# The dilated branch's projection moved ahead of the grouped-query heads

## What is computed

```python
def hybrid_mixer(h, ...):
    proj = h @ w_in                      # 1024 x 8192: dilated qkv | B's q, k, v | gates
    o_a = dilated attention, 3 groups x 8 heads of 64, merged by their log-sum-exp     # S x 512
    o_b = gqa_axial_attention(...)       # 8 query heads, 2 kv heads of 128: rmsnorm, axial rope,
                                         # softmax, values                              # S x 1024
    gates = sigmoid(pg + b_gate)         # S x 2 x 1024
    merged = gates[:, 0] * (o_a @ w_branch_a) + gates[:, 1] * (o_b @ w_branch_b)
    return merged @ w_out
```

## Time and profile before

| | us |
|---|---|
| median of 3 runs | 2217.85 |
| lowest, highest | 2215.59, 2220.27 |
| profiled execution, span from its first to its last instruction | 2216.1 |
| PE busy | 2087.5 (94%) |
| DVE busy | 1321.9 (60%) |
| ACT busy | 924.7 (42%) |
| POOL busy | 191.5 (9%) |
| chain that ended last: PE, DVE, ACT | 84%, 11%, 3% |

### The profile page before, as it was taken

How to read it: one execution, slowest core, us unless ns; L and a number is a source line. 1 busy time by engine, 2 the same in 40 slices (tenths; PEclk the granted TensorE clock), 3 DMA queues, 4 the chain that set the end, 5 groups by cost and what they waited for, 6 DMA issues and landing times.

```text
span 2216.1 us, 29141 instructions
## 1 busy us (share of the span) xinstructions
PE 2087.5 (94%) x12208; PEld 1800.8 (81%) x12208; DVE 1321.9 (60%) x1269; ACT 924.7 (42%) x866; POOL 191.5 (9%) x76
## 2 busy tenths in 40 slices
PE   8999999978999879999999999989989999699998
PEld 7987888876888657887988788879979878687997
DVE  6766656687666635656756666664454556444544
ACT  5344333365333433333335433343444445444433
POOL 0001000121000113001000200010010003311000
PEclk9999999979999999999999999999999999999999
DMA  8443555434554404554544455525446543243552
GB/s 309 153 166 138 209 189 190 157 114 152 190 189 166 158 22 167 190 189 152 209 152 177 154 192 189 190 95 207 182 156 227 146 136 117 74 153 124 187 208 98
DMA packets 32362, 364.16 MB, mean 164 GB/s; under 512 B 3677, under 2 KB 3938, under 8 KB 10130
## 3 DMA queue, kind: packets, MB, share of 16 engines
q1 hardware_dynamic: 28146, 347.49, 42.8%
q0 software_dynamic: 4128, 15.39, 2.7%
HBM read 361.77 MB, written 1.10 MB: 164 GB/s over the span
## 4 chain that ended last, share of the span: by engine, by line
PE 84%; DVE 11%; ACT 3%; issue 1%; DMA 0%; SPq 0%; DVEq 0%; ACTq 0%
PE acc L861 25%; PE bank L1262 10%; PE bank L821 9%; PE bank L823 9%; PE bank L822 9%; PE bank L1264 5%; PE bank L848 2%; PE bank L850 2%; PE bank L849 2%; DVE h L2151 2%; PE bank L1372 1%; PE bank L931 1%; PE bank L1021 1%; PE bank L814 1%; DVE h L2138 1%
## 5 line engine op out<-in xcount | busy, mean ns | idle before, releaser
L821 PE MATMUL bank<-ht_both,w_hi 128*128 128x256 f32 x1696 | 478.3, 282 | 7.0 <-DVE ob_lo L2661 6.8
L823 PE MATMUL bank<-ht_both,w_lo 128*128 128x256 f32 x1696 | 475.4, 280 | 0.0
L822 PE MATMUL bank<-ht_both,w_hi 128*128 128x256 f32 x1696 | 475.0, 280 | 0.0
L2078 DVE TENSOR_TENSOR w_lo<-raw,w_hi 128x4096 fp32r<-128x4096 f32 (+3 forms) x87 | 327.9, 3769 | 137.2 <-ACT w_hi L1525 136.9
L1513 ACT ACTIVATE w_hi<-raw 128x2048 fp32r<-128x2048 f32 x174 | 323.4, 1908 | 143.4 <-PE bank L823 138.6
L1262 PE MATMUL bank<-ht_both,w_hi 128*128 128x512 f32 x1024 | 359.7, 394 | 0.5
L1525 ACT ACTIVATE w_hi<-raw 128x4096 fp32r<-128x4096 f32 (+3 forms) x87 | 269.0, 3093 | 185.3 <-PE bank L1264 175.1
L821 PEld LDWEIGHTS bank<-ht_both,w_hi 128*128 128x128 f32 x1696 | 320.2, 189 | 12.2 <-issue 11.2
L822 PEld LDWEIGHTS bank<-ht_both,w_hi 128*128 128x128 f32 x1696 | 320.1, 189 | 1.6 <-issue 0.5
L823 PEld LDWEIGHTS bank<-ht_both,w_lo 128*128 128x128 f32 x1696 | 320.2, 189 | 0.0
L2073 DVE TENSOR_TENSOR w_lo<-raw,w_hi 128x2048 fp32r<-128x2048 f32 x98 | 220.1, 2287 | 115.4 <-ACT w_hi L1513 115.3
(11 more groups left out here) (325 smaller groups left out, 2999.9 us busy)
## 6 DMA issues: line engine op xcount, KB each, us to landing
raw<-slabs_in SPq DMA_DIRECT2D x147, 2048.0 KB, 7.7
raw<-slabs_in SPq DMA_DIRECT2D x23, 1024.0 KB, 6.3
raw<-slabs_in SPq DMA_DIRECT2D x12, 512.0 KB, 10.0
g_tab<-gains_in POOLq DMA_DIRECT2D x11, 512.0 KB, 6.5
a_bias<-bias_rows POOLq DMA_DIRECT2D x8, 576.0 KB, 6.9
b_tab<-gains_in POOLq DMA_DIRECT2D x8, 512.0 KB, 7.7
raw<-slabs_in SPq DMA_DIRECT2D x2, 1152.0 KB, 5.7
raw<-slabs_in SPq DMA_DIRECT2D x1, 1280.0 KB, 7.1
```

What stands on the lines that cost most here:

```text
L821: nc.tensor.matmul(o, whi, xhi, start=first, stop=False)
L822: nc.tensor.matmul(o, whi, xlo, start=False, stop=False)
L823: return nc.tensor.matmul(o, wlo, xhi, start=False, stop=last)
L2078: nc.vector.tensor_tensor(w_lo[slot][:, 0:w], raw[slot][:, 0:w], w_hi[slot][:, 0:w].bitcast(F32), ALU.subtract).then_inc(lo_ready, 1)
```

## The change

PE computes wa right after gates 0 to 3, ahead of bt and of branch B's heads, and puts it into the four accumulator banks, which stand in the list `bank` as numbers 4 to 7. There it stays until DVE reads it at the place where it did before. The slab of wa moves from place 16 to place 14; the slabs of gates 4 to 7 move from 14 and 15 to 15 and 16. ACT gets a second split between gates 3 and bt (slab 15), so that it splits slab 16 at head 0, 17 at head 4, 18 at head 7, and the split after the sigmoid goes. DVE's and POOL's lists are as before: POOL still makes the low parts of places 13 to 17, now gates, wa, gates, gates, wb.

```diff
--- before.py
+++ after.py
@@ -50,6 +50,7 1941.00:1947.00 6.00, 5.68 (x35) 5.71 (x36) 2.40 (x9) 1.02 (x4) 0.00 (x0) 0.72 0.73 303
 FFN_B = D_FF2 // 256
 A_G, A_H, A_HD = 3, 8, 64
 AV_SLAB = (3, 4, 8)
+GATE_SLAB = (12, 13, 15, 16)
 B_H, B_KV, B_HD = 8, 2, 128
 B_SCALE = B_HD ** -0.5
 SLAB = 4096
@@ -308,6 +309,7 1941.00:1947.00 6.00, 5.68 (x35) 5.71 (x36) 2.40 (x9) 1.02 (x4) 0.00 (x0) 0.72 0.73 303
         bank = [ctx.enter_context(nc.psum_tensor(f"bank{i}", [P, 512], F32)) for i in range(4)]
         acc = [[ctx.enter_context(nc.psum_tensor(f"acc{t}{n}", [P, 512], F32)) for n in range(2)]
                for t in range(TT)]
+        bank += acc[0] + acc[1]
 
 
         cst_loaded = sem("cst_loaded")
@@ -321,8 +323,8 1941.00:1947.00 6.00, 5.68 (x35) 5.71 (x36) 2.40 (x9) 1.02 (x4) 0.00 (x0) 0.72 0.73 303
         hi_ready = sem("hi_ready")
         lo_ready = sem("lo_ready")
         slab_used = sem("slab_used")
-        bank_full = [sem(f"bank_full{i}") for i in range(4)]
-        bank_read = [sem(f"bank_read{i}") for i in range(4)]
+        bank_full = [sem(f"bank_full{i}") for i in range(8)]
+        bank_read = [sem(f"bank_read{i}") for i in range(8)]
         acc_full = sem("acc_full")
         acc_half = sem("acc_half")
         acc_read = sem("acc_read")
@@ -410,7 +412,7 1941.00:1947.00 6.00, 5.68 (x35) 5.71 (x36) 2.40 (x9) 1.02 (x4) 0.00 (x0) 0.72 0.73 303
         BESIDE_M = {0: [("qn", 2), ("qr", 1)], 1: [("rot", 2)], 2: [("qn", 3), ("mv", 0, 1)], 3: [("mv", 1, 1)]}
 
 
-        uses = [0] * 4
+        uses = [0] * 8
         ticket = {}
         turn_of = [0]
 
@@ -535,6 +537,8 1941.00:1947.00 6.00, 5.68 (x35) 5.71 (x36) 2.40 (x9) 1.02 (x4) 0.00 (x0) 0.72 0.73 303
             take("ao", hd)
         for i in range(4):
             take("gt", i)
+        for i in range(4):
+            take("wa", i, slot=4 + i)
         for i in range(5):
             take("bt", i)
         take("bs", 0)
@@ -546,8 +550,6 1941.00:1947.00 6.00, 5.68 (x35) 5.71 (x36) 2.40 (x9) 1.02 (x4) 0.00 (x0) 0.72 0.73 303
             take("bp", hd)
             if hd % 2 == 0:
                 take("bo", hd // 2)
-        for i in range(4):
-            take("wa", i)
         for i in range(4):
             take("wb", i)
         take_transposes(2 * DEPTH + 2, aligned=True)
@@ -632,8 +634,8 1941.00:1947.00 6.00, 5.68 (x35) 5.71 (x36) 2.40 (x9) 1.02 (x4) 0.00 (x0) 0.72 0.73 303
             released[g0 + AV_SLAB[i]] = full("av", i, 1)
             released[g0 + 9 + i] = full("b", i, 1)
         for i in range(4):
-            released[g0 + 12 + i] = full("gt", 2 * i + 1)
-        released[g0 + 16] = full("wa", 3)
+            released[g0 + GATE_SLAB[i]] = full("gt", 2 * i + 1)
+        released[g0 + 14] = full("wa", 3)
         for i in range(2):
             released[g0 + 17 + i] = full("wb", 2 * i + 1)
         by_down([g0 + 19, g0 + 20], 2 * DEPTH + 2)
@@ -1345,9 +1347,10 1941.00:1947.00 6.00, 5.68 (x35) 5.71 (x36) 2.40 (x9) 1.02 (x4) 0.00 (x0) 0.72 0.73 303
                     tokens(("b", s, t), g0 + 9 + s, t, 512, KD, 512, 0, ht_hi, ht_lo)
 
                 def gates(i):
-                    need(g0 + 12 + i // 2)
+                    g = g0 + GATE_SLAB[i // 2]
+                    need(g)
                     c = i % 2 * 256
-                    up_pair(("gt", i), g0 + 12 + i // 2, (c, c + P), KD, 512, ht_hi, ht_lo)
+                    up_pair(("gt", i), g, (c, c + P), KD, 512, ht_hi, ht_lo)
 
                 def beside(hd, i):
                     if hd in BESIDE_A:
@@ -1412,6 +1415,11 1941.00:1947.00 6.00, 5.68 (x35) 5.71 (x36) 2.40 (x9) 1.02 (x4) 0.00 (x0) 0.72 0.73 303
 
                 for i in range(4):
                     gates(i)
+                need(g0 + 14)
+                for hd in range(A_H):
+                    pe.wait_ge(*read("ao", hd))
+                for i in range(4):
+                    up_pair(("wa", i), g0 + 14, (i * 256, i * 256 + P), 4, D, oa_hi, oa_lo)
                 for i in range(5):
                     key = ("bt", i)
                     wait_free(*key)
@@ -1458,11 +1466,6 1941.00:1947.00 6.00, 5.68 (x35) 5.71 (x36) 2.40 (x9) 1.02 (x4) 0.00 (x0) 0.72 0.73 303
                                              b_pt[hd % 2][:, kb * S:(kb + 1) * S], start=kb == 0, stop=kb == 1)
                     if hd % 2 == 1:
                         m.then_inc(bank_full[ticket["bo", hd // 2][0]], 1)
-                need(g0 + 16)
-                for hd in range(A_H):
-                    pe.wait_ge(*read("ao", hd))
-                for i in range(4):
-                    up_pair(("wa", i), g0 + 16, (i * 256, i * 256 + P), 4, D, oa_hi, oa_lo)
                 for i in range(4):
                     pe.wait_ge(*read("bo", i))
                 for s in range(2):
@@ -1955,7 +1958,7 1941.00:1947.00 6.00, 5.68 (x35) 5.71 (x36) 2.40 (x9) 1.02 (x4) 0.00 (x0) 0.72 0.73 303
                         .then_inc(b_std, 1)
                 for i in range(4):
                     gates(i)
-                    if i == 1:
+                    if i % 2 == 1:
                         split_one()
                 for i in range(5):
                     copy_bank(("bt", i), b_qk[:, 2 * i:2 * i + 2, :].rearrange("p a s -> p (a s)"))
@@ -1994,7 +1997,6 1941.00:1947.00 6.00, 5.68 (x35) 5.71 (x36) 2.40 (x9) 1.02 (x4) 0.00 (x0) 0.72 0.73 303
                     for i in range(4 * branch, 4 * branch + 4):
                         act.wait_ge(*read("gt", i))
                     nc.scalar.activation(gate[:, c, :], gate[:, c, :], ACT.Sigmoid).then_inc(gate_ready, 1)
-                split_one()
                 for s in range(2):
                     for i in range(2):
                         q = 2 * s + i
@@ -2847,8 +2849,9 1941.00:1947.00 6.00, 5.68 (x35) 5.71 (x36) 2.40 (x9) 1.02 (x4) 0.00 (x0) 0.72 0.73 303
                 parts += columns(qk) + [chunks(dil[:, 2, 0:2, half].reshape(D, 512))]
                 if half == 0:
                     parts.append(chunks(dil[:, 2, 2].reshape(D, 512)))
-            parts += columns(w[:, 3 * A_G * 512:])
-            parts += rows(a["w_branch_a_2"][0]) + columns(a["w_branch_b_2"][0]) + rows(a["w_out_2"][0])
+            own = columns(w[:, 3 * A_G * 512:])
+            parts += own[0:5] + rows(a["w_branch_a_2"][0]) + own[5:7]
+            parts += columns(a["w_branch_b_2"][0]) + rows(a["w_out_2"][0])
     widths, _ = slab_widths()
     slabs = np.zeros((len(widths), P, SLAB), np.float32)
     for g, part in enumerate(parts):
```

## The result

| | before | after |
|---|---|---|
| median of 20 runs, us | 2216.74 | 2221.48 |
| lowest, highest | 2214.19, 2220.27 | 2219.83, 2224.03 |
| span of the profiled execution | 2216.1 | 2219.9 |

The ratio is 1.0021 with a 95% interval of 1.0014 to 1.0027: the change costs 4.7 us, where +1.3 was forecast, on the border of the 0.2% that counted as no change; the interval leaves 1 out. The time lies within the range of 2213.5 to 2223.0. The kernel before is at 2216.74 over 20 runs, 1.1 us under the three runs that the forecast started from.

The account below looks back on a forecast made before the run. The prediction took DVE's rope, partly held up by POOL's subtraction, to bound the stretch around PE's hole. +8.7 us on the rope and -7.4 us behind the heads gave +1.3 us on 2217.85: 2219.2 us, range 2213.5 to 2223.0.

Parts of the forecast that it names:

- rope's second tile, 1883.38 to 1890.75 before: DVE's rope on the second tile of tokens: POOL's two halves of slab 15 hold it up, +8.7 us.
- POOL's start behind the tile's start: POOL starts slab 15 at 1883.7, 0.3 us behind the start of the rope's second tile.
- wa in front of bt: Behind gates 3: wa's 96 matmuls take 11.5 us and are completely hidden in PE's wait for the rope.
- PE's idle time behind wa: Between wa and bt: PE idles about 5 us until the rope ends.
- clock in bt: In bt, behind the gap after wa: clock assumed low again, no difference; staying high would give back about 1.3 us.
- heads, from the scores to the end of the last ob_lo: Branch B's heads: nothing changes in relation to their start, 0 us.
- behind the heads, by starting wb right after the last ob_lo: With wa gone, wb starts at 1957.38 instead of 1964.74, behind a 3.8 us wait: -7.4 us.
- stretch: From the start of the last oa_lo to w_out's first matmul; the forecast's net change of +1.3 us is set against it.
- with or without one fall: Main case, collision and net +1.3 us: 2218 to 2221 us whether or not PE's clock falls once; chance 0.70.
- rival C: Clock falls in PE's waits, notably ahead of wb: one makes +3.0 us, two +4.7 us, 2222.6 us; chance 0.13.
- A: The forecast itself: POOL's slab 15 collides with the rope's second tile, net +1.3 us; chance 0.70.
- The margins of 1.8 and 1.9 us: Behind the heads: slab 18 ready 1.8 us before wb's second half, slab 19 1.9 us before w_out, so neither delays PE.

Follow-up runs that it names:

- e5: Changed kernel with dummy matmuls in PE's waits, three each ahead of gates 5 and gates 7, four ahead of wb: 2219.35 us, 1.0010 of the kernel before.
- e6: Changed kernel with slab 15's low part by DVE and 4 + 3 + 3 dummy matmuls in PE's waits: 2209.21 us, 0.9973 of the kernel before.
- e7: Changed kernel with low parts of slabs 14 and 15 by DVE and 4 + 3 + 3 dummy matmuls: 2209.09 us, 0.9969 of the kernel before.
- e10: Changed kernel with low parts of slabs 14 to 17 by DVE and four dummy matmuls ahead of wb: 2202.52 us, 0.9936 of the kernel before.
- e1: Changed kernel with slab 15's low part made by DVE behind the rope's second tile instead of by POOL: 2214.98 us, 0.9989 of the kernel before.
- e2: Kernel before with only the early split of slab 15 behind gates 3, wa left behind the heads: 2225.85 us, 1.0037 of the kernel before.

## Why the prediction was right, and where it was off

The terms of the sum against the changed kernel's profile, in us:

| step | forecast | measured |
|---|---|---|
| rope's second tile, 1883.38 to 1890.75 before | +8.7 | 1882.25 to 1898.43: +8.8 |
| POOL's start behind the tile's start | 0.3 | 0.27 |
| wa in front of bt | 11.5, hidden | 11.0, hidden |
| PE's idle time behind wa | about 5 | 5.78 |
| clock in bt | low again | low again; bt to scores 4.99 against 4.98 |
| heads, from the scores to the end of the last ob_lo | 0 | +1.4: gates 5 +2.9, gates 6 +0.2, gates 7 -1.5, waits -0.2 |
| behind the heads, by starting wb right after the last ob_lo | -7.4 | -7.2: wb starts 0.36 behind ob_lo's end, not 0.15 (0.36 to 0.40 in e5, e6, e7 and e10 too, at a clock of 1.00) |
| wb | 0 | 24.8 against 22.6: +2.2 |
| stretch | +1.3 | +5.3 |

**The mechanism was right.** The hole of PE belonged to DVE's rope, the rope to POOL in part, and moving one slab's split from head 0 to gates 3 brings both of its halves onto the second tile. That the term came out to 0.1 us rests on reading the first tile's rows as an experiment that the kernel had already done: the same operations once with POOL beside them and once without. e1 and e2 show it from both sides.

**The step that failed** is the clock, "with or without one fall" in the forecast and the whole of rival C. It failed three times. First, the fall ahead of wb was treated as one of several that may come or not, but came in all four profiles that have the bare wait. Secondly, a fall was priced at 1.7 us, by the one at gates 7; the one ahead of wb costs 2.2 us in the changed kernel. Thirdly, "in the heads nothing changes" was given without a term for the clock: they had a new and longer fall at gates 5 (+2.9) where the one at gates 7 went (-1.5). The kernel before has one fall behind these waits and the changed one has two, so C needed one more than before, not two, and 0.13 was little for it. C is not a second mechanism beside A: it is A with the clock.

**What is owed to luck.** The forecast of +1.3 is 3.4 us off; the time lies in the range because that was drawn to take in C, and the measured +4.7 us is C's +4.7 only by its sum, since C had two falls of 1.7 us more. With the dummies in the waits (e5) the stretch is at the forecast +1.3, and that is chance in part: the fall of the kernel before at gates 7 is missing (-1.5), wb has the shorter time between matmuls (-0.8), and the first scores ran longer at the lower clock (+1.6). The timed runs of e5 are at +2.3, with an interval of +0.2 to +4.2 us.

The margins of 1.8 and 1.9 us that were worked out for slabs 18 and 19 held: PE had no wait within wb or at w_out. So did the claim that the banks and the wait for the dilated heads cost nothing.

What stays open: why the clock falls at gates 5 in one profile for twice as long as in another (0.66 against 0.83 over 10 us, at waits of 3.27 and 3.15 us), and how the falls vary over the timed executions, of which each kernel has one profile only. Why wb's matmuls come every 0.114 us in some profiles and every 0.118 us in others at the same granted clock is open as well. And the span grew by 3.8 us where the stretch grew by 5.3: 1.1 us of this is the earlier entry into the stretch, 0.4 is not accounted for.

## What to carry to other kernels

Before work is moved into a hole of the busiest engine, ask whose the hole is, and what the move sends into the work that ends it: here a slab's split went along with the projection, and what filled the hole with 11 us also lengthened it by 9. When an operation is six times as long in one place as in another, look at what GpSimd does beside it; a subtraction that VectorE does in 4.5 us of its own idle time can be cheaper than one that GpSimd does for nothing. Work that covered a wait leaves it bare when it is moved away, and its price is then the idle time and the slow clock after it; a few dummy matmuls that end before the wait does buy the second part back.

## What was not expected of the hardware

A stream of ten VectorE operations, queued without a wait between them, did not keep GpSimd out: GpSimd began 0.27 us after the first had begun, and the stream took 11.52 us instead of 2.7. The Trainium skill, SBUF — State Buffer, section "Who interferes with whom", has the block for the whole of an instruction, and the traces agree; they add that between two instructions of a stream the waiting engine gets its turn. A small VectorE operation is held up as well: 128x2 elements took 3.21 us instead of 0.17. And the clock of TensorE stayed at its lower level (1.2 GHz) after the wait had ended: in the changed kernel the mean from 1963 to 1973 is 0.66, with TensorE busy without a gap from 1966.70 on, where the first 21 matmuls take 4.6 us.
